# Expert weights in transfers of 2 MB: one DMA fills two neighbouring slots of the weight ring

## What is computed

```python
def moe_swiglu(h, router, w_gate, w_up, w_down):
    ...
    for e in range(N_EXPERTS):                      # 8 experts, D_FF_EXPERT = 2048
        out = out + gates[:, e:e + 1] * swiglu(ht, w_gate[e], w_up[e], w_down[e])
    return out.reshape(bsz, seq, d)
```

## Time and profile before

| | |
|---|---|
| time, median of 3 runs (lowest, highest) | 2086.67 us (2085.4, 2086.81) |
| span of the profiled execution | 2084.0 us |
| PE busy | 2046.0 us, 98% of the span |
| DVE busy | 1409.6 us, 68% |
| ACT busy | 1198.0 us, 57% |
| transfers of a full slab | 427, 1024 KB each |
| HBM read over the span | 461.11 MB, 224 GB/s |

### The profile page before, as it was taken

The page is one execution under the profiler, slowest core; times in us unless marked ns, Lnnn a source line. Parts: engine busy times, 40 slices in busy tenths (PEclk is TensorE's granted clock), DMA queues, the critical chain, the costliest instruction groups (busy, mean ns, idle before and its releaser), DMA issues.

```text
span 2084.0 us, 27770 instructions
## 1 busy us (share of the span) xinstructions
PE 2046.0 (98%) x10189; PEld 1713.0 (82%) x10189; DVE 1409.6 (68%) x1529; ACT 1198.0 (57%) x1374; POOL 93.9 (5%) x140
## 2 busy tenths in 40 slices
PE   9999999999999999999999999999999999999999
PEld 9988887778878878787788877888888899888887
DVE  6655457698888988889444685445555579785444
ACT  4454458677777777776344565444444465874442
POOL 1010001000000000010100010000000000220000
PEclk9999999999999999999999999999999999999999
DMA  8555434389999999998555443555455455445551
GB/s 305 187 183 185 180 140 145 122 326 362 361 362 370 357 362 351 367 384 339 183 185 194 160 164 145 185 195 184 178 184 181 147 180 194 162 152 182 190 192 41
DMA packets 68267, 467.11 MB, mean 224 GB/s; under 512 B 7776, under 2 KB 8176, under 8 KB 13520
## 3 DMA queue, kind: packets, MB, share of 16 engines
q1 hardware_dynamic: 63616, 455.24, 59.0%
q10 hardware_dynamic: 3536, 8.10, 1.2%
q0 software_dynamic: 1024, 2.56, 0.5%
HBM read 461.11 MB, written 4.75 MB: 224 GB/s over the span
## 4 chain that ended last, share of the span: by engine, by line
PE 84%; DVE 6%; ACT 5%; issue 3%; DVEq 1%; ACTq 0%; POOL 0%; POOLq 0%
PE gu L2146 15%; PE gu L2148 15%; PE gu L2147 15%; PE acc L2146 9%; PE acc L2148 9%; PE acc L2147 9%; DVE wlo L1303 3%; ACT whi L710 2%; PE acc L2242 2%; PE acc L2244 2%; PE acc L2243 2%; PE tp L2256 1%; PE tp L2175 1%; PE acc L2696 1%; PE tp L2728 1%
## 5 line engine op out<-in xcount | busy, mean ns | idle before, releaser
L1303 DVE TENSOR_TENSOR wlo<-raw,whi 128x2048 fp32r<-128x2048 f32 (+2 forms) x435 | 987.1, 2272 | 365.6 <-ACT whi L710 365.2
L710 ACT ACTIVATE whi<-raw 128x2048 fp32r<-128x2048 f32 (+1 forms) x436 | 827.4, 1899 | 214.5 <-PE acc L2148 165.9
L2146 PE MATMUL gu<-whi,actA_hi 128*128 128x512 f32 (+1 forms) x1448 | 575.4, 397 | 3.6 <-DVE actA_lo L1324 1.5
L2147 PE MATMUL gu<-wlo,actA_hi 128*128 128x512 f32 (+1 forms) x1448 | 563.0, 389 | 1.3 <-issue 1.3
L2148 PE MATMUL gu<-whi,actA_lo 128*128 128x512 f32 (+1 forms) x1448 | 564.0, 389 | 0.0
L2146 PEld LDWEIGHTS gu<-whi,actA_hi 128*128 128x128 f32 x1448 | 272.0, 188 | 59.8 <-issue 5.3
L2148 PEld LDWEIGHTS gu<-whi,actA_lo 128*128 128x128 f32 x1448 | 271.7, 188 | 59.1 <-issue 1.5
L2147 PEld LDWEIGHTS gu<-wlo,actA_hi 128*128 128x128 f32 x1448 | 272.4, 188 | 52.0
L2146 PE MATMUL acc<-whi,hT_hi 128*128 128x512 f32 x656 | 256.6, 391 | 4.4 <-DVE wlo L1303 4.1
L2148 PE MATMUL acc<-whi,hT_lo 128*128 128x512 f32 x656 | 255.6, 390 | 0.0
L2147 PE MATMUL acc<-wlo,hT_hi 128*128 128x512 f32 x656 | 255.4, 389 | 0.0
(11 more groups left out here) (448 smaller groups left out, 2257.2 us busy)
## 6 DMA issues: line engine op xcount, KB each, us to landing
raw<-in_slabs SPq DMA_DIRECT2D x427, 1024.0 KB, 4.9
y_rows<-big ACTq DMA_DIRECT2D x7, 512.0 KB, 7.4
raw<-in_slabs SPq DMA_DIRECT2D x4, 576.0 KB, 3.7
hT_hi<-cum_rows ACTq DMA_DIRECT2D x8, 256.0 KB, 3.1
hT_lo<-cum_rows ACTq DMA_DIRECT2D x8, 256.0 KB, 4.3
raw<-in_slabs SPq DMA_DIRECT2D x2, 768.0 KB, 4.1
raw<-in_slabs SPq DMA_DIRECT2D x2, 640.0 KB, 3.9
x<-in_x SPq DMA_DIRECT2D x2, 512.0 KB, 4.8
```

What stands on the lines that cost most here:

```text
L710: act.activation(whi[:, n0 % SPLIT, 0:w], raw[:, n0 % RAW, 0:w], ACT.Copy).then_inc(slab_hi, 1)
L1303: dve.tensor_tensor(wlo[:, n0 % SPLIT, 0:w], raw[:, n0 % RAW, 0:w], whi[:, n0 % SPLIT, 0:w].bitcast(F32), ALU.subtract).then_inc(slab_spli ...
L2146: pe.matmul(o, xh, wh, start=start, stop=False)
L2147: pe.matmul(o, xh, wl, start=False, stop=False)
```

## The change

In the expert stage SP issues `load_pair` for the slabs with numbers s, s+1 where s is even: slabs 64 and 65, 66 and 67, up to 252 and 253, 95 transfers of 2 MB in place of 190 of 1 MB. The first slab (63) and the last (254) stay single. A pair fills slots (0, 1), (2, 3) or (4, 5). It waits until the old content of both slots is consumed (`slab_split` at s + 2, where the single load of s waited for s + 1), and its landing counts up the semaphore of its first slot alone. The source is read as "o p n -> p o n": for each partition two pieces of 8 KB that lie 1 MB apart. ACT waits for that semaphore ahead of the first slab of a pair and for nothing ahead of the second, whose waits on `raw_full` are left out; later counts on these semaphores are lowered by the number of seconds so far. DVE, PE and the data are the same, and no other stage is touched.

```diff
+            def load_pair(s, slot):
+
+                sp.wait_ge(slab_split, s + 2)
+                sp.dma_start(raw[:, slot:slot + 2, :], a["slabs"][bass.ds(s, 2)].rearrange("o p n -> p o n")
+                             ).then_inc(raw_full[slot], 16)
+
+            def expert_loads(f):
+
+                n = 3 * f.C
+
+                def pairs(k0, k1, ex):
+                    for k in range(k0, k1, 2):
+                        load_pair(f.s0 + k + n * ex, (f.s0 + k) % RAW)
+                load(f.s0, f.s0 % RAW, SLAB)
+                pairs(1, 2, 0)
+                with sp.Fori(0, f.experts - 1) as ex:
+                    pairs(3, n + 2, ex)
+                pairs(3, n - 1, f.experts - 1)
+                load(f.s0 + n * f.experts - 1, (f.s0 + n * f.experts - 1) % RAW, SLAB)
+
...
-                if f.kind == "ffn":
+                if f.kind == "ffn" and f.gates is not None:
+                    expert_loads(f)
+                elif f.kind == "ffn":
                     ffn_loads(f)
...
+            f, = [f for f in stages_used if f.kind == "ffn" and f.gates is not None]
+            assert (f.s0 + 1) % 2 == 0
+            second_of_pair = range(f.s0 + 2, f.s0 + 3 * f.C * f.experts - 1, 2)
+
+            def seconds_before(n0):
+
+                return sum(n < n0 and n % RAW == n0 % RAW for n in second_of_pair)
+
             def split_hi(base, k, i, per):
 
                 n0 = base + k
-                act.wait_ge(raw_full[n0 % RAW], 16 * (n0 // RAW + 1) + 16 * i + 16 * per)
+                n = n0 + (RAW * per if isinstance(per, int) else 0)
+                if n not in second_of_pair:
+                    act.wait_ge(raw_full[n0 % RAW], 16 * (n0 // RAW + 1 - seconds_before(n)) + 16 * i + 16 * per)
                 act.wait_ge(slab_used, n0 + 1 + RAW * i + RAW * per)
```

## The result

The changed kernel takes 2090.83 us in the median of 9 runs (2088.75 to 2093.27), the kernel before 2085.87 us (2085.34 to 2087.02). The ratio is 1.0025, with a 95% interval of 1.0016 to 1.0034: slower by 5.0 us. The forecast was 2088.5 us in a range of 2083 to 2097, and a change of under 0.2% (4.2 us). The time lies inside the range; the change of 5.0 us is just past that bound. The profiled execution is the slowest of the nine (2093.27 us, with a span of 2091.5).

The account below looks back on a forecast made before the run. PE was taken to bound the expert stage, with transfers early. Span 2084.0 + 1.8 at the gathers + 0 for the other 94 pairs = 2085.8; the median lies 2.7 above, so 2088.5 us, range 2083 to 2097.

Parts of the forecast that it names:

- signs of being right: Expert stage: pairs land in 7.3 to 8.5 us, ACT waits for DMA only near 940 us, stage 1.5 to 2 longer.
- sign of being wrong: Expert stage: landings of pairs longer than 9.6 us, or the time falling by over 4 us.
- What bounds the kernel: Expert stage: PE sets the pace at 8.41 us per three slabs, DVE follows closely, and transfers come early.
- Rival 3: Expert stage: larger transfers make landings steadier and help after all, 2082 us as a typical case; chance 0.10.
- Issues and ACT's waits worth nothing: Expert stage: halving SP's 190 issues hides behind its waits, and dropping 95 ACT waits gains nothing.
- The 9.6 us for a landing: Undisturbed turn of the slab ring: time from a pair's issue at 614.4 until ACT wants its first slab at 624.01.
- With 7.9 the first slab lands 1.7 us early: Undisturbed ring turn: a pair landing in 7.9 us is early by 1.7 for its first slab, 4.5 for its second.
- The term: Expert stage away from the gathers: the other 94 pairs add 0 us.
- Rival 1: Expert stage: pairs land too late everywhere; at landings of 10.5 us, 14 us lost and 2103 in all; chance 0.20.
- The pair lands no earlier; the later issue may add up to 0.5: At the gathers: one pair lands at 943.9, its first split 1.5 us late, 1.5 to 2.0 lost with later issue.
- Rival 2: Pair loads: two pieces per partition 1 MB apart are read slower; at 350 GB/s some 18 us, 2105; chance 0.06.
- The sign that I had named: Sign for slow distant pieces: a transfer rate under 400 GB/s from 935 to 960 us.

Follow-up runs that it names:

- the first trace: Profiled execution of the changed kernel's first measurement, the slowest of its nine: 2093.27 us, with a span of 2091.5.
- the second trace: Profile of the changed kernel measured again unaltered on another chip, where its median was 2090.31 against 2085.58 us for the kernel before.
- the last expert single: Changed kernel with pairs in the first seven experts and single transfers in the last: 2087.14 against 2085.72 us; with a pair's slabs packed side by side, 2086.9 against 2085.95.
- The joint landing alone: Kernel before, single transfers requested as early as before, but ACT waits for both slabs of a pair ahead of the first: 2087.56 against 2085.72 us.
- adjacent pieces: Changed kernel with a pair's two slabs packed side by side in HBM, 16 KB contiguous per partition: 2096.33 us against 2085.72 for the kernel before.

## Why the forecast was near, and which steps were off

**The number: near, in part by luck.** The sum held 1.8 us of loss, and 5.0 were measured. Of the 3.2 us that it lacked, 0.8 were made up by its base: 2086.67 us, the median of three runs, where nine give 2085.87. Most of the prediction's signs of being right failed: pairs landed in 8.9 us and not in 7.3 to 8.5, ACT waited for 24 of them and not only near 940 us, and the part up to slab 235 alone cost 3.4 us in the first trace (0.2 in the second). Its sign of being wrong, landings over 9.6 us, holds for 40 of the 95 pairs in the first trace and 20 in the second.

**What bounds the kernel: right.** PE sets the pace. DVE, ACT and PE cost the same per instruction after the change. Rival 3, a gain from larger transfers, found nothing: each of the ten runs was slower in its median than the kernel before, six of them beyond their intervals.

**Issues and ACT's waits worth nothing: not contradicted.** The two runs with 85 pairs and the last expert single have 85 issues and 85 waits less than the kernel before, and are at +1.4 and +1.0 us. What a single issue or wait is worth was not tried by itself.

**The 9.6 us for a landing: right.** Waits appear in the spell of 10.6 us and not in that of 7.5. In the first trace no pair that landed in 9.5 us or less was waited for. One slab less of it costs 38.1 us, 33 more than the change itself.

**"With 7.9 the first slab lands 1.7 us early": mis-sized.** Landings of pairs were 8.9 us in the median, 8.6 from 450 to 925 us in the second trace and 9.1 in the first, and over 10 in spells. I had taken the value of a single's landing in one stretch for all, and 422 GB/s, which the earlier trace rows show during the gathers, for the reserve everywhere. In the spell, from 565 to 595 us, the engines were 98% busy at 374: no reserve over PE's demand. The term was 0 for the other pairs; the run with the last expert single measures 1.4 us, in an interval that holds no change. Rival 1 is thus true in spells, at a tenth of its 14 us.

**"The pair lands no earlier; the later issue may add up to 0.5": the step that failed.** 1.8 us were forecast for the gathers, 3.8 measured. The joint landing alone cost what I had worked out (1.8; 1.3 in its trace). I had priced one pair, where five are late, and had kept today's landing of the second slab, as if the request didn't matter once the engines are full. It does when another queue shares them. In the second trace this pair was issued at 933.0, only 0.3 us after the single of the earlier trace rows, and landed at 946.6, 2.7 us after it. The gathers bring 2.1 MB, 5.0 us of the engines' time at 422 GB/s. In the 20 us from the first issue to the last landing the path can move 8.4 MB and PE wants 7.5. That leaves 0.9 MB for 2.1, and the slabs are 1.2 MB or about 3 us of PE's pace behind. This is an estimate from the earlier trace rows and the gathers' landings. The queues bear it out: from 940 to 945 us the slabs of the changed kernel got 1.45 MB (the lines are in the last section), which is 290 GB/s where PE wants 374. Singles meet it with 4.5 us of margin and keep about 1.2; pairs meet it with 1.7 or less (0.4 for slab 238, the last before the waits), and five in a row are late. One gather in place of four removes the waits but for 1.1 us; 2.1 MB more of traffic gives singles the same ones. That the gathers' share is the cause is shown by these two runs, most plainly in their traces: from slab 235 to 255 they fall behind by 0.0 us with one gather, and singles by 4.2 (1.7 of it the clock) with more traffic. The split of the loss into microseconds is arithmetic.

**Rival 2, distant pieces: not borne out.** Packing them together didn't shorten a landing. The sign that I had named, under 400 GB/s from 935 to 960 us, did come up (385), but it was badly chosen: singles with the joint landing move 398 there, and the last 5 us of the window, where the engines are only 64% busy, pull the mean down (416 to 428 from 940 to 955 us). The Trainium skill, DMA: Bandwidth & Descriptors, section Latency and other measured facts, has copies with rows 4 MiB apart at 103 GB/s, half of the 214 of padded ones; here the partitions are read 8 KB apart, and no run shows such a loss.

**Open.** What makes a spell of slow landings isn't settled. They go with the stores of the results, but two executions of the same kernel, with the same stores, had 14.5 and 3.1 us of waits before 925 us. No version beats the kernel before: in this stage it never waits for a landing, so no transfer scheme has anything to give back.

## What to carry to other kernels

Ask of a ring of buffers by how many microseconds each landing is early, and price a larger transfer by what it takes from that: one slab of later request plus one slab of joint landing, here some 5 us where singles were 4.5 early. A transfer that is hidden gains nothing from being larger, and the loss begins where other traffic shares the engines, so look at the margin there and not in the steady part. When one half of an edit is harmless and the other nearly so, the two together may still cost, because a margin is spent once.

## What the hardware showed that I had not expected

Long packets hold up another queue. With 16 KB per packet of slabs the gathers of 4 KB rows landed in 18.0 us, with 8 KB in 13.0 to 13.1. The Trainium skill, DMA: Bandwidth & Descriptors, section Queues, rings and completion order, says that each DMA engine takes turns between its queues packet by packet; the trace agrees. From 940 to 945 us the queue of the slabs (q1) and that of the gathers (q0) move the same number of packets, first in the changed kernel, then with adjacent pieces (packets, MB, share of the engines):

```profile
q1 hardware_dynamic: 190, 1.45, 68.8%
q0 software_dynamic: 189, 0.69, 33.8%
...
q1 hardware_dynamic: 121, 1.72, 80.4%
q0 software_dynamic: 121, 0.43, 21.1%
```

Packet for packet, the queue with the longer packets gets more of the bytes: the gathers' part falls from 0.69 to 0.43 MB in the same 5 us.

The rate of busy engines varies, and not with the company. It was 422 GB/s with gathers and slabs together, and still 421 from 945 to 950 us of the kernel before, when the gathers had landed and the slabs were alone. From 575 to 590 us, with slabs alone and the engines 99% busy, it was 365 in the changed kernel and 380 in the kernel before. What makes the difference isn't shown.

A PE that runs dry can pay twice. Where it had been busy for only part of 5 us (3.04, 2.62, 3.30 and 1.41 in the stretches named above, 3.96 ahead of the one from 985 to 990 us), its granted clock was at 1.2 in place of 2.4 GHz for about 3.4 us, or 7 in the case of 1.41. One such stretch cost 1.6 us where it could be read by itself. It doesn't follow each time: from 945 to 950 us of the changed kernel PE is busy for 3.76 us, and the clock stays at 1.00.
